# Hybrid layers: the convolution moved into the projections, index scores and top-k behind it, the last block's top-k between the heads

## The reference

```python
z = rmsnorm(x, mix_norm) @ w_in
(aq, ak, av, iq, ik, iw, bq, bk, bv, bg, br, cu, dcq, dckv, dkpe) = jnp.split(...)
# index scores of a block of 128 queries, and the top-k mask of the attention branch A
s = relu(einsum('bthd,bsd->bths', iqb, ik) * idx_scale)      # 8 index heads
score = where(causal, einsum('bths,bth->bts', s, wb), -inf)
_, sel = lax.top_k(score, 128)
# branch C: gate, causal depthwise convolution with 31 taps over 256 channels
a, gate = jnp.split(cu, 2, axis=-1)
h = conv(a * sigmoid(gate), w_dw) + b_dw
y_c = silu(rmsnorm(h, c_norm))
# branch D: 4 query and 4 key heads of width 96, each normed and rotated (rope)
```

## Time and profile before

| what | value |
| --- | --- |
| median of 3 runs | 3665.62 us |
| profiled execution, its time / its span | 3664.48 us / 3662.7 us |
| busy PE, DVE, ACT, POOL | 94%, 44%, 32%, 17% of the span |
| chain that ended last | PE 87%, DVE 8%, ACT 2%, issue 2%, POOL 1% |
| first hybrid layer: projections, gates to heads, heads | about 415 to 568, 572 to 591, 591 to 637 us |
| the same of the second layer | 1129.8 us later |

### The profile page before, as it was taken

The page is one execution under the profiler, slowest core; times in us unless marked ns, Lnnn a source line. Parts: engine busy times, 40 slices in busy tenths (PEclk is TensorE's granted clock), DMA queues, the critical chain, the costliest instruction groups (busy, mean ns, idle before and its releaser), DMA issues.

```text
span 3662.7 us, 39900 instructions
## 1 busy us (share of the span) xinstructions
PE 3445.2 (94%) x14476; PEld 2613.6 (71%) x14476; DVE 1625.0 (44%) x2220; ACT 1172.1 (32%) x1728; POOL 611.8 (17%) x388
## 2 busy tenths in 40 slices
PE   7999997999999999998899999899799997879997
PEld 5888763678887888765577888565578875558886
DVE  3332388443323332368644332834433327453323
ACT  4232334433323332334333321213333223443322
POOL 1110234111100110033211100401211004331101
PEclk9999998899999999999799999899899999989999
DMA  4332320023333332331013333340133332223332
GB/s 131 97 92 97 81 75 31 1 70 92 95 94 92 92 96 94 81 80 60 1 41 92 93 96 92 82 84 29 46 92 95 94 92 64 69 60 95 92 97 69
DMA packets 419549, 286.04 MB, mean 78 GB/s; under 512 B 57352, under 2 KB 395116, under 8 KB 419308
## 3 DMA queue, kind: packets, MB, share of 16 engines
q1 hardware_dynamic: 418624, 283.62, 26.7%
q10 hardware_dynamic: 828, 1.13, 0.1%
HBM read 280.24 MB, written 4.47 MB: 78 GB/s over the span
## 4 chain that ended last, share of the span: by engine, by line
PE 87%; DVE 8%; ACT 2%; issue 2%; POOL 1%; DMA 0%; ACTq 0%; DVEq 0%; SPq 0%; POOLq 0%
PE bank L838 24%; PE bank L839 24%; PE bank L840 24%; PE bank L1221 1%; PE bank L1104 1%; PE bank L1105 1%; PE bank L833 1%; PE bank L1123 1%; DVE arena L2017 1%; DVE x L2162 1%; PE bank L1215 1%; DVE arena L1996 1%; DVE small L1993 1%; PE bank L974 0%; PE bank L973 0%
## 5 line engine op out<-in xcount | busy, mean ns | idle before, releaser
L840 PE MATMUL bank<-xn_lo,w_hi 128*128 128x512 f32 x2800 | 1099.9, 393 | 0.0
L838 PE MATMUL bank<-xn_hi,w_hi 128*128 128x512 f32 x2496 | 998.4, 400 | 66.9 <-DVE x L2162 41.7
L839 PE MATMUL bank<-xn_hi,w_lo 128*128 128x512 f32 x2496 | 989.8, 397 | 0.0
L1901 DVE TENSOR_TENSOR w_lo<-wring,w_hi 128x1024 fp32r<-128x1024 f32 x434 | 535.7, 1236 | 908.1 <-ACT w_hi L1467 907.6
L1467 ACT ACTIVATE w_hi<-wring 128x1024 fp32r<-128x1024 f32 x490 | 517.8, 1059 | 1162.8 <-DMA wring<-in_ffn_down 357.6
L840 PEld LDWEIGHTS bank<-xn_lo,w_hi 128*128 128x128 f32 x2800 | 530.2, 189 | 133.0
L838 PEld LDWEIGHTS bank<-xn_hi,w_hi 128*128 128x128 f32 x2496 | 470.2, 188 | 186.9 <-issue 68.6
L839 PEld LDWEIGHTS bank<-xn_hi,w_lo 128*128 128x128 f32 x2496 | 471.2, 189 | 103.9 <-issue 1.4
L839 PE MATMUL bank<-h_hi,w_lo 128*128 (+1 forms) x1056 | 419.6, 397 | 0.0
L840 PE MATMUL bank<-h_lo,w_hi 128*128 (+1 forms) x1056 | 416.5, 394 | 0.0
L838 PE MATMUL bank<-h_hi,w_hi 128*128 (+1 forms) x1056 | 415.4, 393 | 0.0
(11 more groups left out here) (373 smaller groups left out, 3263.1 us busy)
## 6 DMA issues: line engine op xcount, KB each, us to landing
wring<-in_ffn_gate SPq DMA_DIRECT2D x88, 512.0 KB, 3.7
wring<-in_ffn_up SPq DMA_DIRECT2D x88, 512.0 KB, 3.7
wring<-in_ffn_down SPq DMA_DIRECT2D x88, 512.0 KB, 3.5
wring<-in_ffn_w_gate SPq DMA_DIRECT2D x44, 512.0 KB, 3.8
wring<-in_ffn_w_up SPq DMA_DIRECT2D x44, 512.0 KB, 3.7
wring<-in_ffn_w_down SPq DMA_DIRECT2D x44, 512.0 KB, 3.5
wring<-in_w_in SPq DMA_DIRECT2D x34, 512.0 KB, 3.8
wring<-in_w_out SPq DMA_DIRECT2D x16, 512.0 KB, 4.2
```

The costliest lines, as they stand in the source:

```text
L838: nc.tensor.matmul(ps, w_hi[:, slot, t, 0:M], hi, start=start, stop=False)
L839: nc.tensor.matmul(ps, w_lo[:, slot, t, 0:M], hi, start=False, stop=False)
L840: return nc.tensor.matmul(ps, w_hi[:, slot, t, 0:M], lo, start=False, stop=stop)
L1901: nc.vector.tensor_tensor(w_lo[:, slot, :, :].rearrange("p k c -> p (k c)"), wunit[:, slot, :], w_hi[:, slot, :, :].rearrange("p k c -> p ...
```

## The change

The order of the units is new: the four units of the convolution's inputs come first, then those of the index, the attention's queries and keys, and branch D, and at last B. All 24 index products now follow the units `dcq1` to `bk`, four behind each. POOL's two multiplications into `hpad` move up accordingly. DVE's stream in the projections becomes: all 62 taps, first those of one channel tile and then those of the other, each waiting for the one directly before it; then all 24 score additions and the three masks; then the rounds of block 3 and of block 2. The 16 rounds of block 1 stand between the heads, two in each of 8 steps, where 31 taps stood.

```diff
-Z_LABELS = ["iq0", "iq1", "ik", "misc", "aq0", "aq1", "ak0", "ak1", "br0", "br1", "cg0", "cg1", "ca0", "ca1", "dcq0", "dcq1",
-            "dckv", "bq", "bk"]
+Z_LABELS = ["cg0", "ca0", "cg1", "ca1", "iq0", "iq1", "ik", "misc", "aq0", "aq1", "ak0", "ak1", "dcq0", "dcq1", "dckv",
+            "br0", "br1", "bq", "bk"]
...
-    if _u >= 4:
-        for _ in range(2):
+    if _u >= Z_LABELS.index("dcq1"):
+        for _ in range(4):
...
-                act.e.wait_ge(conv.h, conv.by(act.l, 2 * TAPS - 1 + ct))
+                act.e.wait_ge(conv.h, conv.by(act.l, TAPS * (ct + 1)))
...
+        def dve_top(dve, tb, first, end):
+            for r in range(first, min(end, TOP_N)):
+                nt = (3 - tb) * TOP_N + r
...
+                nc.vector.max(m8, score(tb)).then_inc(top_max.h, 1)
+                dve.e.wait_ge(top_max.h, top_max.by(dve.l, nt + 1))
+                nc.vector.match_replace(score(tb), m8, score(tb), SENTINEL).then_inc(top_rep.h, 1)
...
+        def dve_conv(dve):
+            for n in range(2 * TAPS):
+                ct, j = n // TAPS, n % TAPS
+                if j == 0:
+                    dve.e.wait_ge(hp_ready.h, hp_ready.by(dve.l, ct + 1))
...
-                    dve.e.wait_ge(conv.h, conv.by(dve.l, n - 1))
+                    dve.e.wait_ge(conv.h, conv.by(dve.l, n))
...
-                dve_conv(dve, CONV_EARLY + i * CONV_PART, CONV_EARLY + (i + 1) * CONV_PART)
+                dve_top(dve, 1, 2 * i, 2 * i + 2)
...
-                dve_index(dve)
-                dve_conv(dve, 0, CONV_EARLY)
+                dve_conv(dve)
+                dve_scores(dve)
+                dve_top(dve, 3, 0, TOP_N)
+                dve_top(dve, 2, 0, TOP_N)
                 dve_mixers(dve)
...
-                    if n == Z_LABELS.index(f"ca{ct}") + 3:
+                    if n == Z_LABELS.index(f"ca{ct}") + 2:
```

More of the change, by code:

```diff
@@ L1967, in add_half, with dve_scores @@
                                            op0=ALU.mult, op1=ALU.add).then_inc(x_ready.h, 1)
-        def dve_index(dve):
-            ni = nt = 0
+        def dve_scores(dve):
+            ni = 0
             for tb in (3, 2, 1):
-                N = (tb + 1) * P
                 for h in range(IDX_HEADS):
@@ L1976, in dve_index @@
                     w = wA[:, tb * 8 + h:tb * 8 + h + 1]
-                    r = idx_r[ni % 4][:, 0:N]
+                    r = idx_r[ni % 4][:, 0:(tb + 1) * P]
                     if h == 0:
@@ L1985, in dve_index @@
                     ni += 1
-                dve.e.wait_ge(idx_acc.h, idx_acc.by(dve.l, ni))
+            for tb in (3, 2, 1):
+                dve.e.wait_ge(idx_acc.h, idx_acc.by(dve.l, IDX_HEADS * (4 - tb)))
                 dg = score(tb)[:, tb * P:]
                 nc.vector.tensor_tensor(dg, dg, C("causal"), ALU.add).then_inc(idx_mask.h, 1)
-                dve.e.wait_ge(idx_mask.h, idx_mask.by(dve.l, 4 - tb))
-                for r in range(TOPK // 8):
-                    if r:
-                        dve.e.wait_ge(top_rep.h, top_rep.by(dve.l, nt))
-                    nc.vector.max(m8, score(tb)).then_inc(top_max.h, 1)
-                    nt += 1
-                    dve.e.wait_ge(top_max.h, top_max.by(dve.l, nt))
-                    nc.vector.match_replace(score(tb), m8, score(tb), SENTINEL).then_inc(top_rep.h, 1)
@@ L1997, in dve_index @@
-                dve.e.wait_ge(top_rep.h, top_rep.by(dve.l, nt))
-                nc.vector.tensor_scalar(score(tb), score(tb), 0.9 * SENTINEL, NEG, ALU.is_gt, ALU.mult).then_inc(top_done.h, 1)
-        CONV_EARLY = 31
-        CONV_PART = -(-(2 * TAPS - CONV_EARLY) // 9)
-        def dve_conv(dve, first, end):
-            if first == 0:
-                dve.e.wait_ge(hp_ready.h, hp_ready.by(dve.l, 2))
-            for n in range(first, min(end, 2 * TAPS)):
-                j, ct = n // 2, n % 2
-                w = cur_dw[:, n:n + 1]
+        TOP_N = TOPK // 8
@@ new lines, in dve_top @@
+        def dve_top(dve, tb, first, end):
+            for r in range(first, min(end, TOP_N)):
+                nt = (3 - tb) * TOP_N + r
+                if r:
+                    dve.e.wait_ge(top_rep.h, top_rep.by(dve.l, nt))
+                else:
+                    dve.e.wait_ge(idx_mask.h, idx_mask.by(dve.l, 4 - tb))
+                nc.vector.max(m8, score(tb)).then_inc(top_max.h, 1)
+                dve.e.wait_ge(top_max.h, top_max.by(dve.l, nt + 1))
+                nc.vector.match_replace(score(tb), m8, score(tb), SENTINEL).then_inc(top_rep.h, 1)
+                if r == TOP_N - 1:
+                    dve.e.wait_ge(top_rep.h, top_rep.by(dve.l, nt + 1))
+                    nc.vector.tensor_scalar(score(tb), score(tb), 0.9 * SENTINEL, NEG, ALU.is_gt, ALU.mult).then_inc(top_done.h, 1)
@@ L2011, in dve_conv @@
+        def dve_conv(dve):
[3 more added lines that the diff above has]
+                    dve.e.wait_ge(hp_ready.h, hp_ready.by(dve.l, ct + 1))
+                w = cur_dw[:, 2 * j + ct:2 * j + ct + 1]
                 src = hpad[:, ct, j:j + SEQ]
```

## The result

The changed kernel takes 3693.39 us (median of 4 runs, 3691.92 to 3694.97), the kernel before beside it 3665.88 (4 runs, 3665.03 to 3668.38): a ratio of 1.0075, 95% interval 1.0063 to 1.0087. It is slower by 27.5 us. Forecast was 3707, slower by 41, with a range from 3678 to 3740. The two profiled executions have spans of 3662.7 and 3693.2 us, 30.5 apart.

A forecast was written before the change was run, and what follows sets the result against it. PE was taken to bound the kernel (87% of the chain), so only its waits could move. Terms +31.2 - 1.55 + 4.4 - 13.0 = +21 us a layer, +42 in two, on 3664.5 gave 3707, range 3678 to 3740.

The forecast's parts named there:

- The end of the taps: Projections, first layer: DVE's 62 taps, met by 14 POOL splits, start at 434.3 and end at 515.4.
- the pitch of a dependent tap: Taps in sequence stand 0.85 us apart instead of 0.665 interleaved, so each costs 0.18 us more.
- The stall: Projections: the fifth ReLU waits behind all taps; PE idles about 9 us and loses 4 by its clock, 12.6 together.
- the old one: Projections before the change: PE's 4.46 us wait for ACT's ReLU plus clock loss, 8 to 9 us in all.
- The first rival: Taps in sequence keep the interleaved pitch of 0.665 us: taps end at 502, PE's stall goes, 3682 us; chance 12%.
- From the last addition to the gates: 8.8 us from `bk` to the rounds, then 45.1 us of rounds: gates at 603.6 instead of 572.37, +31.2.
- Gates to first head: From the gates to the first head's scaling: -1.55 for a wait that goes, +4.4 for PE's lower clock.
- The wait of 1.55 us: DVE's wait for the Ln behind its early taps before the change; forecast to go, -1.55 us.
- The heads: Two rounds replace four taps and fit a gap of 2.9 us: pitch 4.2 us, 33 us against 46.1, -13.
- the lower clock in the heads: PE stays at half clock through the heads, 58 us instead of 33: 3761 in both layers, 3734 in one; chance 14%.
- rounds that don't fit: Rounds between the heads cost 2.6 us each beside the loop, so the heads gain nothing: 3742 us; chance 4%.
- The faster one: No stall and PE at full clock from first dv product to attention, if gates start before 593: 3653 us; chance 4%.

The follow-up runs named there:

- e1: The changed kernel with the taps of the two channel tiles interleaved again, tile 0 seven ahead: 3680.26 us.
- e4: The changed kernel with 8 instead of 16 rounds for each of blocks 3 and 2: 3652.27 us.
- e2: The changed kernel with block 2's rounds between the heads and block 1's ahead of the gates: 3684.24 us.
- e6: The changed kernel with interleaved taps, index products behind each unit from aq0 on, DVE's stream in small portions, six taps behind the norms: 3618.11 us.
- e7: e3 with its last 8 taps moved behind the norms, where DVE waits for the first head: 3660.39 us.
- e3: The kernel before with only block 1's rounds moved between the heads and all 62 interleaved taps ahead of the gates: 3653.44 us.
- e5: The changed kernel with 29 fp32 matmuls, results unread, in PE's idle ahead of the dv products: 3683.87 us.

## Why the prediction was right, and where its terms were off

**The end of the taps: 511.8 instead of 515.4.** They started at 434.08, as reckoned (434.3), and met the 14 splits reckoned. The term that was mis-sized is the pitch of a dependent tap. DVE's timeline of the kernel after has three taps of which the second meets the split of 453.37, and four that no split meets:

```profile
452.50 4.35 DVE L2020 SCALAR_TENSOR_TENSOR arena<-hpad,cur_dw,arena 128x512 f32<-128x512 f32 x3
...
479.63 3.12 DVE L2020 SCALAR_TENSOR_TENSOR arena<-hpad,cur_dw,arena 128x512 f32<-128x512 f32 x4
```

With 0.75 us for the last tap, the four start (3.12 - 0.75) / 3 = 0.79 us apart. The prediction had taken 0.85 from additions and called it a distance between taps; the earlier trace rows have it for additions alone. So dropping the interleaving adds 0.79 - 0.665 = 0.13 us to a tap and not 0.18. In the first row the split adds 4.35 - 0.75 - 2 x 0.79 = 2.0 us, as reckoned. 62 x 0.79 + 14 x 2.0 + 0.9, less 0.5 for the two first taps, makes 77.4 us; measured are 77.7. The 0.06 us too much per tap make up the 3.6 us. The splits are stretched too where they meet a tap, as POOL's timeline shows by two of them:

```profile
434.00 2.42 POOL L2549 TENSOR_TENSOR w_lo<-wring,w_hi 128x1024 fp32r<-128x1024 f32 x1
...
453.37 2.93 POOL L2549 TENSOR_TENSOR w_lo<-wring,w_hi 128x1024 fp32r<-128x1024 f32 x1 [3.03 <-ACT w_hi L1467]
```

**The stall: right in kind, half in size.** The fifth ReLU waited for DVE behind all taps, 5.03 us, and PE 5.45 instead of 9. The clock loss behind it was 0.25 of 7 us, 1.8, instead of 4. Together 7.3 us instead of the 12.6 charged: of the 5.4 us too much, 3.2 are the idle, through the taps' end, and 2.2 the clock. The new stall replaces the old one, as said. The Trainium skill (VectorE: DVE Perf Modes, The DRAIN you can't avoid), which the prediction weighed, says that the semaphore costs nothing extra. What I made of it, that taps in sequence cost what interleaved ones do, is not so here: they start 0.79 and 0.665 us apart, and interleaving gave 13 us in e1. The first rival had put taps at the old pitch to an end at 502 and the kernel to 3682 us; e1, which has that pitch for 48 of its 62 taps, has 502.85 and 3680.26.

**From the last addition to the gates: right.** 8.8 us were reckoned from `bk` to the rounds, and it was 552.47 - 543.92 = 8.6; the rounds 45.1, and it was 597.36 - 552.47 = 44.9. The gates came at 597.36 instead of 603.6, early by what the stall was smaller and by 0.4 us more. e4 showed that these 45 us are paid one to one.

**Gates to first head: +2.1 in place of +2.85, by two errors that cancel.** That this sum is near is luck. The wait of 1.55 us went, as said. The norms took 6.60 us instead of the 4.7 of before: they now meet POOL's gated keys, of which I had not thought. The clock cost 1.7 us instead of 4.4, since from 615 on, ahead of the first scaling, it was at 1.00. The 1.7 are the dv products, 3.65 us here; PE's timeline of before has 1.96, behind a wait of 3.12 us:

```profile
583.33 1.96 PE L1002 MATMUL bank<-arena 128*128 128x256 f32 x8 [3.12 <-DVE arena L2050]
```

**The heads: right.** 651.15 + 0.67 - 618.15 = 33.7 us (33 forecast, 46.1 before); pitch 4.23 as forecast, ended by ACT's Exp; rounds of unchanged length. e2 showed that even the rounds over 384 columns fit. The rivals for the lower clock in the heads and for rounds that don't fit are out. (The latter's sum is loose as well: 13 - 7 x 2.6 is -5.2 us and not nothing, which gives 3743 and not 3742.) The faster one is out by its own condition: it asked for gates before 593. e6, whose gates start at 562, is on the other side of that point and is faster.

**Sum.** Forecast +31.2 - 1.55 + 4.4 - 13.0 = +21 us a layer. Measured in the first: +25.1 to the gates, +2.1 to the first scaling, -12.4 in the heads, -0.7 behind them: +14.1. The terms that were mis-sized are the tap's pitch, 0.79 us instead of 0.85, which is 3.6 us a layer, and the clock behind PE's idles: 2.2 us too much behind the stall and 2.7 behind the long idle, the latter made up for by the norms, 1.9. In the second layer the sum is +15.8, and the two values of the stretches behind the layers added 0.7. So the mechanism was right, and its size too large: 41 us forecast, 27.5 measured, at the lower edge of the 3692 to 3722 that the prediction gave as its own uncertainty.

## What to carry to other kernels

A long chain of operations without waits is not free work in an in-order stream: what it holds up is the small operation behind it that frees a buffer for the others. And what is left to the end of the stream is paid in full: with all index products behind the later units and all additions ahead of the first round, 45 us of rounds came late. Deal such work out in portions sized to the units of the engine that sets the pace; the same operations in that order (e6, with interleaved taps) were 75 us faster than in blocks. And where the pace-setting engine's clock falls in waits, compare two kernels by aligned stretches, those of unchanged code too: a difference of 3 to 8 us may be the clock, which can take a good edit's gain away (e7) or reward one that does nothing (e3, e5).

## What the runs showed of the chip that I had not expected

- A wait of 1.17 us at full PE clock is followed by the half clock for some 7 us in 11 of 22 places, with the same waits and the same matmuls around it, and the 11 are those in which the clock had come back latest behind the first reduction of attention. It costs 3 to 4 us when it is. A wait of 3.88 us behind 25 us of matmuls at full clock (e5) was followed by it too.
- The 29 us idle did not cost more than a wait of 5.77: in the kernel after, from the norms' end to the first scaling, it took 9.6 us, against 7.9 before, and from gates to first scaling 20.8 and 21.5 us, against 21.2 in e4, where the wait was 5.77.
- A tap that waits for the one directly before it starts 0.79 us behind it, one that waits for the last but one 0.66; the additions, which also wait for the one before, stood 0.85 apart.
- The exclusion between DVE and POOL isn't one of two operands alone, as the prediction had it: the first tap, a TENSOR_SCALAR that reads one tensor, took 2.62 us beside a split and 0.54 without. MAX8 and MATCH_REPLACE8 over 512 columns took 0.68 to 0.70 us in either case.
